# Merged up products in two MLPs and a reordered tail in a two-block transformer kernel

## The reference

```
def rms_norm_2(x, g):
    xf = x.astype(jnp.float32)
    y = xf * lax.rsqrt(jnp.mean(xf * xf, axis=-1, keepdims=True) + RMS_EPS)
    return (y * g.astype(jnp.float32)).astype(x.dtype)

def sq_relu_mlp(xn, w1, w2):
    return jnp.square(jax.nn.relu(xn @ w1)) @ w2

    for layer in range(DEPTH_2):
        xn = rms_norm_2(x, norm_mix[layer])
        ...  (even_mixer in layer 0, odd_mixer in layer 1)
        x = x + sq_relu_mlp(rms_norm_2(x, norm_mlp[layer]), mlp_w1[layer], mlp_w2[layer])
    return rms_norm_2(x, norm_final)
```

## Time and profile before

| | us |
|---|---|
| median of three runs | 1198.23 |
| the profiled execution | 1196.97 |
| its span, first to last instruction | 1195.2 |
| PE busy | 1156.0 |
| DVE busy | 754.8 |
| ACT busy | 570.3 |
| first MLP, first up pass to the next stage | 539.6 to 719.4 |
| second MLP, first up pass to the tail | 1006.2 to 1183.5 |
| last pass of PE starts | 1185.76 |

### The profile page before, as it was taken

The page is one execution under the profiler, slowest core; times in us unless marked ns, Lnnn a source line. Parts: engine busy times, 40 slices in busy tenths (PEclk is TensorE's granted clock), DMA queues, the critical chain, the costliest instruction groups (busy, mean ns, idle before and its releaser), DMA issues.

```text
span 1195.2 us, 19183 instructions
## 1 busy us (share of the span) xinstructions
PE 1156.0 (97%) x7495; PEld 1006.1 (84%) x7498; DVE 754.8 (63%) x1071; ACT 570.3 (48%) x782; POOL 112.2 (9%) x107
## 2 busy tenths in 40 slices
PE   6999998899999999999999999999999999999996
PEld 2587776699999887668989989999999988999995
DVE  4588445787654675786455456667666676654653
ACT  4574333543433553664333336665666655333432
POOL 1000051297000070000000000000000000000000
PEclk9999999899999999999999999999999999999999
DMA  9764475977755540709465545554555434745500
GB/s 341 238 240 154 141 281 161 285 241 241 214 168 171 177 97 1 282 1 338 154 211 198 171 109 156 158 140 134 150 158 158 159 138 161 276 160 199 199 12 36
DMA packets 200241, 209.42 MB, mean 175 GB/s; under 512 B 6027, under 2 KB 167190, under 8 KB 199990
## 3 DMA queue, kind: packets, MB, share of 16 engines
q1 hardware_dynamic: 196480, 197.41, 51.3%
q0 software_dynamic: 2928, 9.02, 2.7%
q10 hardware_dynamic: 774, 2.17, 0.5%
HBM read 207.53 MB, written 2.01 MB: 175 GB/s over the span
## 4 chain that ended last, share of the span: by engine, by line
PE 92%; DVE 4%; DMA 2%; ACT 2%; issue 1%; ACTq 0%; DVEq 0%; SPq 0%
PE bank L2273 24%; PE bank L2274 23%; PE bank L2275 23%; PE bank L2085 2%; PE bank L2086 2%; PE bank L2087 2%; PE bank L2030 1%; DMA residual<-in_x_dram 1%; PE bank L2677 1%; PE bank L2135 1%; PE bank L2662 1%; PE bank L2653 1%; PE bank L2687 1%; PE bank L1985 1%; DMA weight_pool<-in_gla_w_in_dram 1%; PE bank L2526 1%
## 5 line engine op out<-in xcount | busy, mean ns | idle before, releaser
L2273 PE MATMUL bank<-hT_high,mlp_up_high 128*128 128x256 f32 x512 | 145.2, 284 | 0.9 <-DVE hT_low L1609 0.9
L2275 PE MATMUL bank<-hT_high,mlp_up_low 128*128 128x256 f32 x512 | 144.9, 283 | 0.0
L2274 PE MATMUL bank<-hT_low,mlp_up_high 128*128 128x256 f32 x512 | 144.9, 283 | 0.0
L2273 PE MATMUL bank<-od_w_high,hT_high 128*128 128x384 f32 x376 | 130.1, 346 | 0.0
L2275 PE MATMUL bank<-od_w_high,hT_low 128*128 128x384 f32 x376 | 126.1, 335 | 0.0
L2274 PE MATMUL bank<-od_w_low,hT_high 128*128 128x384 f32 x376 | 125.8, 334 | 0.0
L1234 DVE TENSOR_TENSOR mlp_down_low<-weight_pool,mlp_down_high 128x2048 fp32r<-128x2048 f32 x32 | 73.3, 2290 | 59.1 <-ACT mlp_down_high L707 59.1
L1234 DVE TENSOR_TENSOR od_w_low<-weight_pool,od_w_high 128x3072 fp32r<-128x3072 f32 x24 | 80.6, 3356 | 41.1 <-ACT od_w_high L707 41.1
L2273 PEld LDWEIGHTS bank<-hT_high,mlp_up_high 128*128 128x128 f32 x512 | 98.1, 192 | 2.8 <-issue 1.9
L2273 PE MATMUL bank<-mlp_down_high,hidden_high 128*128 128x512 f32 x256 | 99.9, 390 | 0.0
L2274 PE MATMUL bank<-mlp_down_low,hidden_high 128*128 128x512 f32 x256 | 99.9, 390 | 0.0
(11 more groups left out here) (391 smaller groups left out, 2730.3 us busy)
## 6 DMA issues: line engine op xcount, KB each, us to landing
weight_pool<-in_mlp_w_dram SPq DMA_DIRECT2D x64, 1024.0 KB, 7.6
weight_pool<-in_od_w_in_dram SPq DMA_DIRECT2D x72, 512.0 KB, 5.3
weight_pool<-in_ffn_w_in_dram SPq DMA_DIRECT2D x44, 512.0 KB, 5.1
weight_pool<-in_mod_w_dram SPq DMA_DIRECT2D x20, 1024.0 KB, 7.9
weight_pool<-in_gla_w_in_dram SPq DMA_DIRECT2D x12, 1024.0 KB, 8.2
weight_pool<-in_ffn_w_out_dram SPq DMA_DIRECT2D x22, 512.0 KB, 6.9
weight_pool<-in_gla_w_out_dram SPq DMA_DIRECT2D x2, 2048.0 KB, 18.1
normed<-in_mod_w_dram POOLq DMA_DIRECT2D x16, 256.0 KB, 5.3
```

The lines of the kernel that those rows point to most:

```text
L2273: mm(out_, left[0], right[0], start=start, stop=False, **flag)
L2274: mm(out_, left[0], right[1], start=False, stop=False, **flag)
L2275: return mm(out_, left[1], right[0], start=False, stop=stop, **flag)
```

## The change

The description given with the change names three parts: the even mixer's output in three passes, merged up products in both squared MLPs, and both token tiles updated ahead of the tail's scaling. The difference between the two kernels holds lines for the last two only.

**Up products.** The high and the low activations are now one tensor, `hT_halves`, and `hT_both[:, k]` reads slice k of both, 256 high columns and 256 low columns that lie 2048 words apart. `up_mm` issues one pass of 512 columns (high weights times both) and one of 256 (low weights times high). The 512 columns fill a bank, so each half of 128 hidden columns gets a bank of its own (`up_bank`: banks 4 and 5, or 6 and 7). Columns 0 to 255 hold the sum of high x high and low x high, columns 256 to 511 high x low. ACT copies columns 256 to 511 of both banks to `act_a`, DVE adds columns 0 to 255, and one SCALAR_TENSOR_TENSOR does the Relu and the square: max(x, 0) x x.

**Tail.** DVE updates both halves of tile 0 and the first of tile 1, then does the one-column `final_mean(0)`, the second half of tile 1, `final_mean(1)`, and then the scalings of both tiles. ACT squares halves (`final_square`); the mean of the first half enters the root of the second as a bias (`final_std`).

```diff
-        hT2 = [view(over(f"hT_{w}", "hT", 2048 * i, 2048), 0, KD, SEQ) for i, w in enumerate(("high", "low"))]
+        hT_halves = over("hT_halves", "hT", 0, 4096)
+        hT2 = [view(hT_halves, 2048 * i, KD, SEQ) for i in range(2)]
+        hT_both = hT_halves[:, :].rearrange("p (w k t) -> p k w t", w=2, k=KD)
+
+        def up_bank(j, part):
+
+            return bank[4 + 2 * (j % 2) + part]
...
-                    act.activation(act_a[:, j % 2, :], bank[4 + j % 2][:, :], ACT.Relu).then_inc(s["ff_act"], 1)
+                    for part in range(2):
+                        ins = act.activation(act_a[:, j % 2, 256 * part:256 * part + 256], up_bank(j, part)[:, 256:512], ACT.Copy)
+                    ins.then_inc(s["ff_act"], 1)
...
-            norm_stats(7, res, s["res_ready"], 24)
+
+            def final_square(t, h):
+
+                act.wait_ge(s["res_ready"], 20 + 2 * t + h + 1)
+                at = NS + 42 + 2 * h + t
+                act.activation(work[:, 20480 + 512 * h:20992 + 512 * h], res[:, t, 512 * h:512 * h + 512], ACT.Square, accum_out=stat[:, at:at + 1])\
+                   .then_inc(s["mean_ready"], 1)
+
+            def final_std(t):
+
+                act.wait_ge(s["mean_ready"], 8 + 2 * t + 2)
+                act.wait_ge(s["final_first"], t + 1)
+                act.activation(stat[:, 185 + t:186 + t], stat[:, NS + 44 + t:NS + 45 + t], ACT.Sqrt, bias=stat[:, 183 + t:184 + t], scale=1.0 / D)\
+                   .then_inc(s["std_ready"], 1)
...
-            def update(n, t):
-
-                for h in range(2):
+            def update(n, t, halves=(0, 1)):
+
+                for h in halves:
...
+                    for part in range(2):
+                        v = act_a[:, j % 2, 256 * part:256 * part + 256]
+                        ins = dve.tensor_tensor(v, v, up_bank(j, part)[:, 0:256], ALU.add)
+                    chain(ins)
                     dve.wait_ge(s["w_used"], st - 1)
-                    split_hidden(j, 512, (act_a[:, j % 2, :], act_a[:, j % 2, :]))
+                    sums = act_a[:, j % 2, :]
+                    split_hidden(j, 512, lambda whole: dve.scalar_tensor_tensor(out=whole, in0=sums, scalar=0.0, in1=sums, op0=ALU.max, op1=ALU.mult))
...
-            norm_scale(7, res, xn, before=lambda t: update(5, t))
+
+            def final_mean(t):
+
+                dve.wait_ge(s["mean_ready"], 8 + 2 * t + 1)
+                dve.tensor_scalar(stat[:, 183 + t:184 + t], stat[:, NS + 42 + t:NS + 43 + t], 1.0 / D, EPS, ALU.mult, ALU.add)\
+                   .then_inc(s["final_first"], 1)
+
+            def final_out(t):
+
+                dve.wait_ge(s["std_ready"], 8 + t + 1)
+                root = stat[:, 187 + t:188 + t]
+                chain(dve.reciprocal(root, stat[:, 185 + t:186 + t]))
+                for h in range(2):
+                    half = slice(512 * h, 512 * h + 512)
+                    dve.scalar_tensor_tensor(out=xn[:, t, half], in0=res[:, t, half], scalar=root, in1=frow[:, half], op0=ALU.mult, op1=ALU.mult)\
+                       .then_inc(s["out_ready"], 1)
+
+            update(5, 0)
+            update(5, 1, (0,))
+            final_mean(0)
+            update(5, 1, (1,))
+            final_mean(1)
+            final_out(0)
+            final_out(1)
...
+            def up_mm(out_, w, k, n):
+
+                mm(out_[:, :], w[0], hT_both[:, k], start=(n == 0), stop=False, skip_group_check=True)
+                return mm(out_[:, 0:256], w[1], hT2[0][:, k, :], start=False, stop=(n == KD - 1), skip_group_check=True)
...
-                            ins = split_mm(bank[4 + j % 2][:, 256 * f:256 * f + 256],
-                                           both(mlU[j % 2], lambda x: x[:, 256 * k + P * f:256 * k + P * f + P]),
-                                           both(hT2, lambda x: x[:, k, :]), n == 0, n == KD - 1)
+                            ins = up_mm(up_bank(j, f), both(mlU[j % 2], lambda x: x[:, 256 * k + P * f:256 * k + P * f + P]), k, n)
```

More of the change, by code:

```diff
@@ L314, in program @@
             oo_hi oo_lo od_ps od_raw od_v rot_ready qkT_ps qkT_out out_ready
-            w_used out_used act_chain dve_chain""".split()
+            final_first w_used out_used act_chain dve_chain""".split()
         s = {n: sem(n) for n in names}
@@ L475, in program @@
         RAW_HI = {3: 2, 4: 6, 5: 10, 6: 14}
-        STD_AT = {0: 0, 1: 2, 2: 4, 7: 8}
+        STD_AT = {0: 0, 1: 2, 2: 4}
         def y_done(n):
@@ L1181, in _ @@
             act.activation(stat[:, 92:93], eps, ACT.Sqrt)
-            norm_stats(7, res, s["res_ready"], 24)
+            def final_square(t, h):
[8 more added lines that the diff above has]
+                   .then_inc(s["std_ready"], 1)
+            final_square(0, 0)
+            final_square(0, 1)
+            final_std(0)
+            final_square(1, 0)
+            final_square(1, 1)
+            final_std(1)
         @block.vector
@@ L1202, in norm_scale @@
                         dve.wait_ge(s["xT_ps"], 4 * n)
-                    if n == 7:
-                        for h in range(2):
-                            half = slice(512 * h, 512 * h + 512)
-                            dve.scalar_tensor_tensor(out=dst[:, t, half], in0=src[:, t, half], scalar=stat[:, at + 4 + t:at + 5 + t],
-                                                     in1=frow[:, half], op0=ALU.mult, op1=ALU.mult).then_inc(s["out_ready"], 1)
-                    else:
-                        dve.tensor_scalar(dst[:, t, :], src[:, t, :], stat[:, at + 4 + t:at + 5 + t], None, ALU.mult)\
-                           .then_inc(s["xn_ready"], 1)
+                    dve.tensor_scalar(dst[:, t, :], src[:, t, :], stat[:, at + 4 + t:at + 5 + t], None, ALU.mult)\
+                       .then_inc(s["xn_ready"], 1)
             def norm_evac(n, dst, gain, shift, order=by_sma, split=False):
@@ L1570, in split_hidden @@
                 whole, hi, lo = act_s[:, j % 2, 0:n], mid2[0][:, j % 2, 0:n], mid2[1][:, j % 2, 0:n]
-                chain(dve.tensor_tensor(whole, *product, ALU.mult))
+                chain(product(whole))
                 chain(dve.tensor_copy(hi, whole))
@@ L1578, in ffn_step @@
                     dve.wait_ge(s["w_used"], f - 1)
-                split_hidden(j, 256, (act_a[:, j % 2, 0:256], bank[4 + j % 2][:, 256:512]))
+                split_hidden(j, 256, lambda whole: dve.tensor_tensor(whole, act_a[:, j % 2, 0:256], bank[4 + j % 2][:, 256:512], ALU.mult))
                 if n_up:
@@ L1796, in update @@
                     ins.then_inc(s["res_ready"], 1)
-                dve.wait_ge(s["res_ready"], 4 * n + 2 * t + 2)
+                dve.wait_ge(s["res_ready"], 4 * n + 2 * t + halves[-1] + 1)
             def mlp_first(l):
@@ L1826, in mlp @@
                 with dve.Fori(0, MLP_LOOPS - 1) as i:
-                    chain.enter(i, 2 * MLP_RING)
+                    chain.enter(i, 3 * MLP_RING)
                     for j in range(MLP_RING):
```

## The result

Over five runs the changed kernel has a median of 1191.71 us (1191.15 to 1192.88), the kernel before 1198.08 us (1196.96 to 1198.72). The ratio is 0.9949, 95% interval 0.9936 to 0.9962: faster by 0.5%, beyond the 0.2% that can be told from no change. Forecast were 1189.4 us and 1186.5 to 1192.0. The profiled execution took 1191.71 us, 1189.9 of it span. The measured median lies 2.3 us above the forecast and 0.3 us inside the upper end of the range.

A forecast was written before the change was run, and what follows sets the result against it. The prediction took PE's pass pace to bound the MLPs, with a DVE, ACT and store tail behind. From the 1198.23 us median, 6.67 for the merge and 2.13 for the tail came off: 1189.4 us, range 1186.5 to 1192.0.

The forecast's parts named there:

- rival C: At round ends in the MLPs: hidden values come late, 0.3 us over at 8 ends, 1191.8 us; chance 0.04.
- The merged up products: Up stages of both MLPs: 512 groups each lose one pass's fixed 0.0133 us, less 0.15 at the starts: -6.67 us.
- The 0.15 us charged for the starts: Start of each MLP: three of four k pairs wait for hT_low and come no earlier, 0.15 us lost.
- The Trainium skill's rule: Up products: a warm gap of N / 2.4 + 2.5 ns would save only 1.3 us, kernel near 1194.8 us.
- ACT's and DVE's added work: 0: Each MLP step: hidden values at most 3.7 us after up instead of 2.51, hidden by 5.26 us of cover; cost 0.
- the shortest cover: End of a round of four: last down's first pass starts 5.26 us behind ACT's start, leaving 1.5 us over.
- The tail: Kernel's end: tile 1's updates move ahead of the scalings, last scaling ends at 1190.6, not 1192.72: -2.1 us (1.6 to 2.4).
- The even mixer: 0: Even mixer's output in three passes: named in the title, but no line of the difference touches it; cost 0.
- Rival A: Up products: each run of 256 pays the 0.0133 us, so the merge gains nothing, 1196.1 us; chance 0.07.
- B: Up products: the load of weights frees the lone 256-column pass, 0.109 instead of 0.120 us, 1183.8 us; chance 0.05.
- D: Merged up pass: the jump of 2048 words breaks the stream, 0.16 us exposed 512 times, +82 us, 1271; chance 0.04.

The follow-up runs named there:

- the simpler tail: Changed kernel with both tiles still updated ahead of the scalings, but whole-tile squares and no one-column mean on DVE: tail 4.35 us, one run 1192.63 us.

## Why the prediction was right, and where it was off

The sign and both mechanisms held: one pass's fixed part goes for each group of three, and the update of tile 1 moves into DVE's idle time. The range held by luck. Measured were 1191.71 us, above the forecast's own range (1187.5 to 1191.3); the range went on to 1192.0 only to take in rival C, a wait that did not occur. The time came out 2.3 us above the forecast because the merge gave 3.27 us less than its term, of which the tail gave 0.36 back. The 0.6 us that are left the other way are within the scatter of the runs.

- **The merged up products.** Forecast -6.67 us, measured -3.40. The step that was mis-sized is "I take 0.2267 and 0.1200, both measured at the same shape": both were read where one length follows itself. In turns the pair lasts 0.3525. Of the fixed 0.0133 us of the pass removed, 0.0058 comes back, and 512 x 0.0075 = 3.84 us are left. Before, the stages took 5.752 us on average and not 5.76, which makes it 3.6. Another 0.3 goes in the 8 down stages behind a double up stage, which take 5.50 us instead of 5.47; why wasn't followed up. The 0.15 us charged for the starts don't show: an MLP's first two up stages are 0.26 us shorter on average, those of later rounds 0.22. The fixed part itself is right: with all merged passes first, the stage is at 5.54.
- **The Trainium skill's rule.** By "TensorE: Matmul & The Clock Gate", "Back-to-back issue gap", the merge would save 1.3 us, an estimate from N / 2.4 + 2.5 ns. The page gives this formula for an isolated matmul, and says that in a stream of weight loads and matmuls both set the spacing, about 131 ns at N = 512; so the prediction compared its stream with a formula that isn't meant for one. Measured were 3.4 us, and with the lengths kept apart 176.25 against 179.43, 6.3 us in both MLPs. Neither figure of the page fits this stream, which has 226.7 ns at 512 columns.
- **ACT's and DVE's added work: 0,** and it was: PE is busy 178.21 of 178.23 us. The latency was put at 3.7 us at most and is 3.35, since two sums in a row take 0.75 us and not 0.84, two of ACT's reads 0.66 and not 0.77, and the gaps less. The prediction called a round's end the shortest cover and said that elsewhere an up stage "lies between, too"; a round's first step has hardly more cover than its last (5.26 to 5.45 against 5.26 us). It cost nothing, and 2.73 us more work made it show.
- **The tail.** Forecast -2.13, measured -2.49. DVE took the last half 0.04 us behind the pass's end instead of 0.10, the reciprocal followed the mean in 0.07, and the second reciprocal was issued while the scaling before it ran. The mean that the forecast charged wasn't fully in the way. The gain is 0.09 above the tail's upper bound of 2.4, as the handovers cost less than was charged. That the squares were halved brings nothing.
- **The even mixer: 0.** Between the MLPs the time is unchanged to 0.03 us, and ahead of the first it differs by 0.6 us, less than that stretch scatters.
- **Rival A** (the merge gains nothing, 1196.1) had the price at the jump; the jump is free and the pair 0.3525, though 44% of the expected gain did go. **B** (0.109 for the lone pass, 1183.8): it fell to 0.117 by start to start, but its neighbour rose from 0.227 to 0.236. **C** (late hidden values, 1191.8) gives nearly the measured time for a wrong reason: there is no such wait in the trace. **D** (the jump breaks the stream) did not happen.

What stays open is why a 512-column pass behind a single shorter one takes about 0.006 us more. By the experiments it is not the jump, the bank or the shared operand, and a longer pass for the load to run beside doesn't lower it. Nor is it the turn from high to low weights, which the three passes of before take as well, at a uniform 0.1200. It is at full size behind one pass of 256 or of 384 columns, about a fifth of that behind two, and not to be seen behind 8 or 16.

The version with all merged passes first beats the kernel before, 0.9930 of it (0.9917 to 0.9944), and its MLPs are shorter than the change's by 2.95 us in sum in the trace. In time its lead over the change is less sure: the change had 0.9959 (0.9945 to 0.9972) beside it but 0.9949 (0.9936 to 0.9962) when first measured, which overlaps. Together with the simpler tail it wasn't run.

## What to carry to other kernels

Take the pace of a pass from rows where it stands between the same neighbours as it will; a pair's pace put together from uniform rows was 2% too short here. When passes are merged for their fixed cost, group those of equal length, if only in twos, and look at which order the first stage's operands arrive in. At the end of a kernel, let the engine that finishes the last result first do all updates and only then the scalings, before refining anything smaller.

## What the runs showed of the hardware

- A stream of 512- and 256-column passes in turn has 0.3525 us a pair instead of 0.3467, at a granted clock of 1.00; of 512 and 384, 0.406 instead of 0.400. By start to start the 512-column pass has 0.236 instead of 0.227 and the 256-column one 0.117 instead of 0.120.
- A moving operand in two runs 2048 words apart costs no more than one in a single run (0.3525 us a pair in both).
- Behind a wait the first pass of PE has its follower after 0.33 us instead of 0.23 (16 waits in one kernel); with the 0.16 us that the profile doesn't count as idle, a wait of 0.98 us cost 1.24.
- At the two MLP starts of one kernel the granted clock fell to 0.50 for 6.8 and 3.4 us when PE had been idle for 2.90 and 2.73 us; where it was idle for 0.55 and 0.38 us it stayed at 1.00. One trace of that kernel, so that the longer wait is the cause isn't shown.
- Two DVE sums of 128x256 with a bank operand take 0.75 us in a row, where one alone has 0.42 in the profile; two of ACT's 256-column reads take 0.66, where one has 0.38.
